# A two-layer hybrid backbone on one core: norms in two parts of the tokens, gating constants loaded during the FFN, two gates first in the merge, output splits ahead of the additions

## The reference: what is computed

```
h  = rms(x) * (1 + scale1) + shift1              # per token norm, per channel modulation (norm 1)
o  = four token mixers of h @ w_in               # neighbourhood, latent, spatial gating, grouped attention
y  = sum_i sigmoid(h @ w_gate[i] + b_gate[i]) * (o[i] @ w_branch[i])        # the merge
x  = x + gate1 * (y @ w_out)                     # the out stage
h2 = rms(x) * (1 + scale2) + shift2              # norm 2
x  = x + gate2 * (silu(g) * a) @ w_down          # a, g = depthwise convolution of h2 @ w_up
```

## Time and profile before

| | |
|---|---|
| Time, median of 3 runs | 2396.87 us (2396.68 to 2398.68) |
| Profiled execution, its own time | 2399.9 us |
| Profiled execution, span | 2398.2 us |
| TensorE busy in it | 95% of the span |
| VectorE, ScalarE, GpSimd busy | 56%, 40%, 7% |
| Granted TensorE clock, mean | 0.985 |
| Moved by DMA | 221.21 MB, mean 92 GB/s |

### The profile page before, as it was taken

One profiled execution on the slowest core, in us unless ns is written; L12 is line 12 of the kernel. 1 busy time (PEld: TensorE's weight loads), 2 busy tenths in 40 slices (PEclk: granted clock), 3 DMA queues, 4 the chain that ended last, 5 costly groups with the idle time before them and its releaser, 6 DMA issues.

```text
span 2398.2 us, 34895 instructions
## 1 busy us (share of the span) xinstructions
PE 2284.1 (95%) x12816; PEld 1891.5 (79%) x12816; DVE 1339.0 (56%) x1877; ACT 955.2 (40%) x1389; POOL 164.9 (7%) x169
## 2 busy tenths in 40 slices
PE   6999988999999989999999979999999998999999
PEld 5788766788888868888888857776778886888887
DVE  6555566466667465425534555556745565645545
ACT  3554556422223253213312345545643334423332
POOL 2113010000000000000000001130100000000000
PEclk9999999999999999999999999999999998999999
DMA  7112110243343211111111131120135542222223
GB/s 281 44 53 71 36 40 19 97 141 132 131 142 126 109 50 65 62 62 62 61 62 62 62 133 44 63 79 18 49 128 177 176 166 90 97 96 97 96 97 114
DMA packets 58621, 221.21 MB, mean 92 GB/s; under 512 B 6720, under 2 KB 6720, under 8 KB 57872
## 3 DMA queue, kind: packets, MB, share of 16 engines
q1 hardware_dynamic: 44496, 160.46, 19.1%
q0 software_dynamic: 14016, 59.26, 6.9%
HBM read 214.45 MB, written 5.24 MB: 92 GB/s over the span
## 4 chain that ended last, share of the span: by engine, by line
PE 88%; DVE 4%; ACT 3%; issue 2%; DMA 2%; ACTq 0%; SPq 0%; DVEq 0%
PE PS L584 85%; PE PS L862 3%; ACT TM L1014 1%; DVE F_lo L1344 1%; ACT XY L1014 1%; DVE ROPE L1400 1%; DMA ROPE<-w_mod 1%; DVE XY L1347 0%; ACT F_hi L1014 0%; DMA SGX<-sg_bs 0%; DVE W_lo L1344 0%; ACT W_hi L1014 0%; DMA XY<-x_spill 0%; DVE XY L1563 0%; DVE TM L1347 0%
## 5 line engine op out<-in xcount | busy, mean ns | idle before, releaser
L584 PE MATMUL PS<-H_hi,W_hi 128*128 128x512 f32 x2240 | 677.7, 359 | 45.1 <-DVE H_lo L1344 26.1
L584 PE MATMUL PS<-H_hi,W_lo 128*128 128x512 f32 x2240 | 670.2, 356 | 0.0
L584 PE MATMUL PS<-H_lo,W_hi 128*128 128x512 f32 x2240 | 668.2, 355 | 0.0
L1344 DVE TENSOR_TENSOR W_lo<-W_st,W_hi 128x1024 fp32r<-128x1024 f32 x278 | 343.7, 1237 | 555.9 <-ACT W_hi L1014 554.4
L1014 ACT ACTIVATE W_hi<-W_st 128x1024 fp32r<-128x1024 f32 x278 | 293.5, 1057 | 820.4 <-PE PS L584 811.2
L584 PEld LDWEIGHTS PS<-H_hi,W_hi 128*128 128x128 f32 x2240 | 370.3, 190 | 121.5 <-issue 44.0
L584 PEld LDWEIGHTS PS<-H_lo,W_hi 128*128 128x128 f32 x2240 | 367.6, 189 | 63.4 <-issue 2.2
L584 PEld LDWEIGHTS PS<-H_hi,W_lo 128*128 128x128 f32 x2240 | 368.5, 189 | 61.8
L584 PE MATMUL PS<-F_hi,W_hi 128*128 128x512 f32 (+1 forms) x952 | 290.1, 359 | 15.9 <-DVEq L442 5.4
L584 PE MATMUL PS<-F_hi,W_lo 128*128 128x512 f32 (+1 forms) x952 | 289.6, 359 | 0.0
L584 PE MATMUL PS<-F_lo,W_hi 128*128 128x512 f32 (+1 forms) x952 | 287.0, 356 | 0.0
(11 more groups left out here) (130 smaller groups left out, 2089.1 us busy)
## 6 DMA issues: line engine op xcount, KB each, us to landing
W_st<-w_all SPq DMA_DIRECT2D x278, 512.0 KB, 3.4
RA<-w_mod POOLq DMA_DIRECT2D x40, 512.0 KB, 3.7
TM<-w_mod POOLq DMA_DIRECT2D x40, 512.0 KB, 3.7
RA<-w_ada SPq DMA_DIRECT2D x8, 512.0 KB, 8.9
XY<-bias_na POOLq DMA_DIRECT2D x2, 1792.0 KB, 8.0
RA<-w_mod SPq DMA_DIRECT2D x6, 512.0 KB, 8.4
XY<-x_in SPq DMA_DIRECT2D x4, 768.0 KB, 11.7
x_spill<-XY POOLq DMA_DIRECT2D x1, 3072.0 KB, 11.0
```

The source lines that it names most:

```text
L584: return nc.tensor.matmul(o, lhsT, rhs, start=start, stop=stop)
L1344: return nc.vector.tensor_tensor(o, a, b, f)
```

## The change

1. `norm` is taken apart. The tokens are divided into two parts (`halves`): at width 768 first the 256 context tokens, then the 512 latent ones; at width 512 two parts of 256. At norms behind output tiles, the last two output tiles (6 and 7) are computed first for the first part (signal `out_half`), then for the second part. Root, products and low parts of the first part are issued by ScalarE and VectorE among the remaining work of these tiles. `E7_BEHIND` and `SPLIT_BEHIND` say after which k the last tile's addition and a split stand.
2. Each k of a norm has one VectorE product with both the root and the scale (`product`), one ScalarE operation that adds the shift and rounds (`high`), and one VectorE operation (`low`) that adds the shift and subtracts the high part. The scratch is a ring of three (`NU`).
3. `two_early_tiles` goes over the first part for both tiles (the second tile wholly behind the first when `late`), then over the second part with the lag of three. The squares of the second part are multiplied inside it.
4. GpSimd issues the gating constants of layer 1 before, and PAR and the spill after, a wait for the last addition; TensorE waits for the constants only ahead of the gating products.
5. The first two gate blocks of a merge come before its first branch block (`MERGE_HEAD`), and `begin` of TensorE stands behind them.
6. In `out_tiles` with a norm behind them all splits stand ahead of the addition and the square.

```diff
+MERGE_HEAD = (1, 2, 0, 3, 4, 5)
+def halves(w):
+    return [(SEQ, CTX), (0, SEQ)] if w == T else [(0, SEQ // 2), (SEQ // 2, SEQ // 2)]
+E7_BEHIND = {T: 4, SEQ: 2}
+SPLIT_BEHIND = {T: 1, SEQ: 0}
...
@@ gpsimd
-                if l:
-                    begin(pool, p0, "pe", "act", "dve")
-                    pool.dma_start(PAR[:, :], par[l]).then_inc(S["par_loaded"], 16)
-                    pool.dma_start(x_spill, XY[:, :]).then_inc(S["x_spilled"], 16)
                 wait(pool, "mask_step", NHEAD * l)
+                wait(pool, "sg_lo", 2 * l)
                 pool.dma_start(SGG, sg_gain[l]).then_inc(S["sg_loaded"], 16)
...
+                if l:
+                    pool.wait_ge(S["down_add"], KT * len(GROUPS) + 2)
+                    pool.dma_start(PAR[:, :], par[l]).then_inc(S["par_loaded"], 16)
+                    pool.dma_start(x_spill, XY[:, :]).then_inc(S["x_spilled"], 16)
@@ tensor, two_early_tiles
+                for h, (s0, sn) in enumerate(halves(w)):
+                    lag = KT if late and h == 0 else 3
+                    for step in range(KT + lag):
+                        for t, k in ((0, step), (1, step - lag)):
...
+                        if late and h == 0 and step == 2:
+                            seven_squares(w, 1)
+                        if late and h == 0 and step == 4:
+                            eighth_square(w, 1)
@@ tensor, merge
+                        if first(i) and u == 0:
+                            for r in range(2):
+                                gate(i, u, r, b + r)
+                            begin(pe, ph, "act", "dve")
+                            branches(i, u, b + 2)
@@ tensor, out_tiles
+                for h, (s0, sn) in enumerate(halves(w)):
+                    for t in (KT - 2, KT - 1):
+                        if h == 0:
+                            have_block(b0 + t)
+                        pe.wait_ge(S[free], base[free] + t - 1 + 2 * h)
+                        for k in range(k_tiles):
...
+                            if h == 1 and t == KT - 2 and k == 2:
+                                base.advance(**norm_counts())
+                                seven_squares(w, 0)
+                                eighth_square(w, 0)
+                        ins.then_inc(S["block_done" if h else "out_half"], 1)
@@ scalar, out_tiles
+                square(KT - 2, 0)
+                load_root_table()
+                square(KT - 1, 0)
+                root(w, 0)
+                for k in range(KT):
+                    high(w, 0, k, tail)
+                    if k == SPLIT_BEHIND[w]:
+                        used(0, 2, b0 + KT - 2)
+                    if k == 1:
+                        square(KT - 2, 1)
+                    if k == E7_BEHIND[w]:
+                        square(KT - 1, 1)
+                        used(0, 2, b0 + KT - 1)
+                root(w, 1)
+                for k in range(KT):
+                    high(w, 1, k, tail)
@@ vector, out_tiles
-                        early = reloads and first(i)
+                        early = tail is not None
...
+                residual(KT - 2, 0)
+                seventh_square(0)
+                residual(KT - 1, 0)
+                root(w, 0)
+                product(w, 0, 0, sc)
+                for k in range(KT):
+                    if k + 1 < KT:
+                        product(w, 0, k + 1, sc)
+                    low(w, 0, k, sh)
+                    if k == 0:
+                        residual(KT - 2, 1)
+                    if k == SPLIT_BEHIND[w]:
+                        used(0, 2, b0 + KT - 2)
+                    if k == 1:
+                        seventh_square(1)
+                    if k == E7_BEHIND[w]:
+                        residual(KT - 1, 1)
+                used(0, 2, b0 + KT - 1)
+                root(w, 1)
+                product(w, 1, 0, sc)
+                for k in range(KT):
+                    if k + 1 < KT:
+                        product(w, 1, k + 1, sc)
+                    low(w, 1, k, sh)
@@ vector, merge
+                        head = first(i) and u == 0
+                        for v in range(3 if head else 1):
+                            used(i, 10, b + v)
```

More of the change, by code:

```diff
@@ L354, in bank, with stat_at @@
             return PS[:, 512 * i:512 * i + 512]
+        def stat_at(w, h):
+            s0, sn = halves(w)[h]
+            at = 3072 + s0 if w == T else (2560, 3584)[h]
+            return PS[:, at:at + sn]
         def colmajor(ap):
@@ L1033, in squares_of_x, with root, high @@
                     split_hi(b, b, 16)
-            def norm(ph, w, sc, sh):
+            def root(w, h):
+                s0, sn = halves(w)[h]
+                act.wait_ge(S["ss"], base["ss"] + h + 1)
+                op(NY0[:, s0:s0 + sn], stat_at(w, h), ACT.Abs_reciprocal_sqrt, bias=EPSB).then_inc(S["y0"], 1)
+                act.wait_ge(S["y0"], base["y0"] + h + 1)
+                op(NRT[:, s0:s0 + sn], NY0[:, s0:s0 + sn], ACT.Square).then_inc(S["y_sq"], 1)
+            def high(w, h, k, sh):
+                s0, sn = halves(w)[h]
+                act.wait_ge(S["norm_u"], base["norm_u"] + KT * h + k + 1)
+                op(H_hi[:, k, s0:s0 + sn], NU[k % 3][:, s0:s0 + sn], ACT.Identity,
+                   bias=MOD[:, stream(s0), sh + k:sh + k + 1]).then_inc(S["norm_hi"], 1)
@@ L1054, in norm @@
-                base.advance(**norm_counts())
+                for h in range(2):
+                    root(T, h)
+                for h in range(2):
+                    for k in range(KT):
+                        high(T, h, k, SH1)
+                base.advance(**norm_counts(False))
             def in_stage(l, ph):
@@ L1226, in split_y, with copies, sigmoid @@
                     op(F_hi[:, k, 0:w], X3[:, k, 0:w], ACT.Copy).then_inc(S["y_hi"], 1)
+                def copies(i, u, b):
+                    for r in range(NBR):
+                        if r < NBR - 1:
+                            act.wait_ge(S["sub_gemm"], i * 6 + (base["sub_gemm"] + 3 * u + r + 1))
+                        else:
+                            used(i, 10, b)
+                        wait(act, "gate_mul", i * 8 + (base["gate_mul"] + NBR * (u - 1) + r + 1)
+                             if not first(i) or u else 0)
+                        op(BR[:, r, 0:w], pair(2 + r % 2, w), ACT.Copy).then_inc(S["br_copy"], 1)
+                def sigmoid(i, u, r, b):
+                    used(i, 10, b)
+                    wait(act, "gate_mul", i * 8 + (base["gate_mul"] + NBR * u + r - 1)
+                         if not first(i) or u or r > 1 else 0)
+                    op(SIG[:, r % 2, 0:w], pair(r % 2, w), ACT.Sigmoid,
+                       bias=PAR[:, bass.ds(i * 2 + (u + C_BG + KT * r), 1)]).then_inc(S["gate_sig"], 1)
                 def body(i, last):
@@ L1430, in in_stage, with first_norm @@
+            def first_norm(ph):
+                begin(dve, ph, "pe", "act")
+                for h in range(2):
+                    root(T, h)
+                for h in range(2):
+                    for k in range(KT):
+                        product(T, h, k, SC1)
+                        if k:
+                            low(T, h, k - 1, SH1)
+                    low(T, h, KT - 1, SH1)
+                base.advance(**norm_counts(False))
             def in_stage(l, ph):
@@ L1678, in body @@
                         ins.then_inc(S[name], 1)
-                        if squares and u == 0 and not first(i):
+                        if tail is not None and u == 0 and not first(i):
                             dve.wait_ge(S["sq"], i * 2 + (base["sq"] + 1))
@@ L1691, in body @@
                             used(i, 2, b0 + u, stop=final and last_phase)
-                def last(i):
-                    return isinstance(i, int) and i == KT // 2 - 1
-                repeat(dve, KT // 2, body, peel_last=last_phase or squares)
+                if tail is None:
+                    repeat(dve, KT // 2, body, peel_last=last_phase)
+                    done[0] += KT
+                    base.advance(**{name: KT})
+                    return
+                repeat(dve, KT // 2 - 1, body)
@@ new lines, in out_tiles, with residual @@
+                sc, sh = tail
+                def residual(t, h):
+                    s0, sn = halves(w)[h]
+                    if h:
+                        dve.wait_ge(S["block_done"], b0 + t + 1)
+                    else:
+                        dve.wait_ge(S["out_half"], base["out_half"] + t - KT + 3)
+                    x = X3[:, t, s0:s0 + sn]
+                    stt(x, pair(t % 2)[:, s0:s0 + sn], MOD[:, stream(s0), gate + t:gate + t + 1], x, ALU.mult, ALU.add
+                        ).then_inc(S[name], 1)
@@ L1751, in _ @@
                     ada()
[L1752 removed]
+                    one_plus_scale(SC1)
                 end(dve, "dve")
```

277 lines of the change are left out of this document (152 added, 125 removed).

## The result

The changed kernel takes 2367.3 us (median of 4 executions, 2365.8 to 2370.6) where the kernel before takes 2397.8 on the same chip: ratio 0.990, 95% interval 0.988 to 0.992, a gain of 30.4 us where 25.4 were forecast. It was measured twice more beside the kernel before: 2369.8 against 2394.0 (ratio 0.990, 0.988 to 0.992) and 2372.7 against 2392.2 (0.991, 0.990 to 0.993), gains of 24.3 and 19.5 us. So the gain is between 19 and 31 us, and part of the first 30 belongs to that comparison and not to the change; where it sits is the last point of the explanation.

The account below looks back on a forecast made before the run. TensorE was taken as the bound, busy 2284.1 of 2398.2 us, so only its gaps count. Gains 8.5 + 8.1 + 1.4 + 2.0 + 5.9 + 1.0 - 1.5 = 25.4 give a median of 2371.5 us, range 2364 to 2384.

Parts of the forecast that it names:

- second norm, layer 0: Halved norm behind layer 0's output tiles: from tile 5's end to the next tile 41.4 us instead of 49.9, gain 8.5.
- first norm, layer 1: Layer 1's first norm, halved and without the wait for gating constants: 42.6 us instead of 50.7, gain 8.1.
- first norm, layer 0: Norm without output tiles to hide under: next tile starts at 75.5 instead of 77.44, gain 2.0 us.
- merge entries: Two gates first in each merge: phase signal waits of 3.0 and 2.4 us shrink to about 0.4, gains 2.5 and 2.0.
- VectorE caught up in the merge: In the merge VectorE starts modulation 10 us later but catches up before branch copies need buffers; otherwise up to 5 us lost.
- splits first: Last down stage of layer 0: the 1.6 us wait for W_lo becomes 0.6 us for residual 0, gain 1.0.
- clock lost in the norms: Halved stretches idle TensorE in short pieces, so its clock may drop: 0 to 1.7 us a norm, 1.5 taken in all.
- B: Rival: thin norm stretches leave TensorE at 1.2 GHz through the early tiles; 2413 us; chance 0.07 with other losses.
- A: Rival: VectorE's queue bounds the norms harder, 0.5 us per 256-column step instead of 0.42; gain 15, 2382 us; chance 0.17.
- C: Rival: the norm's second part ends no earlier than now, only the merge gains 4 to 7; 2391 us; chance 0.08.
- D: Rival: shorter waits inside the first half, first halves entirely hidden; gain 32 to 36, 2362 us; chance 0.06.
- The rule against the change: Skill advice for VectorE pieces of at least 512: norms better whole, halving only a loss of 1.9 us per norm.

Follow-up runs that it names:

- the fourth run: Changed kernel with one more unused 128x256 VectorE product ahead of each of eight first-part products, in the three norms behind output tiles; 2375.3 us.
- the third: Changed kernel with ScalarE's square of tile 7 and the split behind it moved one place back, VectorE's list as it was; 2366.1 us.
- the tenth run: Changed kernel with the second silu right behind the first and three modulation tiles of VectorE ahead of its wait for the merge's third block; 2364.1 us.
- the fifth run: The changed kernel measured again, unedited, beside the kernel before; 2369.8 us against 2394.0.
- the eleventh run: The changed kernel measured a third time, unedited, beside the kernel before; 2372.7 us, ratio 0.9912.
- the first run: Kernel before with only the three gating constant loads moved ahead of the wait for the FFN's end; 2389.1 us against 2393.1.
- four such edits: On the changed kernel: ScalarE's square and split later, odd residuals before splits, two x tiles reloaded early, merge silu and modulation tiles earlier; together 2360.1 us.

## Why the prediction was right

The forecast (2371.5, range 2364 to 2384) held, and at most places for its reasons. That the terms below add up to 24.9 where the forecast has 25.4 is in part luck: 1.5 us for the clock that did not lengthen the norms cancel against 1.3 us for a stop in the merge that the forecast did not have, and 1.1 too much for the first norm against smaller misses the other way. By its own terms, in us, all from the profiled executions:

```
term                               forecast   measured
second norm, layer 0                 8.5        8.4    (49.9 -> 41.5)
first norm, layer 1                  8.1        8.1    (50.7 -> 42.6; constants 4.5, halving 3.6)
second norm, layer 1                 1.4        1.2    (34.8 -> 33.6)
first norm, layer 0                  2.0        0.9    (28.7 -> 27.8)
merge entries                        4.5        4.9    (2.95 + 2.44 idle -> 0.26 + 0.27)
clock at the merge's entry           1.4        1.6
VectorE caught up in the merge       0         -1.3    (472.72 instead of about 465)
splits first                         1.0        1.1    (1.64 -> 0.52)
clock lost in the norms             -1.5        0      (see below)
```

*The walks.* Second norm of layer 0: the wait for tile 5's pair ended at 3.6 (forecast 3.8), residual 7 ran at 18.7 (18.7), the hole lay behind k=4, the second part's first `H_lo` was ready at 28.2 (28.6), the end came at 41.5 (41.4). This part was right because it walked both in-order lists operation by operation; the fourth run shows that the list of VectorE is the price, the third that ScalarE's is close behind it.

*First norm of layer 0*: the term was mis-sized, 0.9 us where 2.0 were forecast. The next tile does start at 75.17, 2.3 us earlier than at 77.44, but 1.4 of that is the start of the whole program: TensorE stopped ahead of the norm at 47.33 in the one execution and at 48.74 in the other. In the kernel before and in the changed one:

```profile
57.20 0.98 PE L584 MATMUL PS<-H_hi,W_hi 128*128 128x512 f32 x2 [8.46 <-DVE H_lo L1344]
```

```profile
52.85 0.55 PE L611 MATMUL PS<-H_hi,W_hi 128*128 128x256 f32 x1 [5.52 <-DVE H_lo L1459]
```

From the start of that idling (48.74; 47.33) to the next tile it is 28.7 and 27.8 us; later executions of the changed kernel have 27.8 as well. The walk has 26.8 on this scale (75.5 - 48.74), 1.0 too short. Its two roots in a row end at 3.0 (51.7) and in the trace at 3.8, its lows at 21.2 (69.9) and in the trace at 21.8, and behind the lows 6.0 us pass where the walk has 5.6. That 75.17 lies so near its 75.5 is luck.

*Merge*: the entry was right, the sentence "it catches up before the branch copies of the next u need their buffers" was not. The buffers were not the next thing needed, the weight split of the sixth block was; the tenth run shows it.

*The clock.* The 1.5 us loss did not come in layer 0 (granted clock 1.00 in every stretch of that norm, with idle pieces of up to 0.8 us). It did come in the two norms of layer 1 (first fence), but not in every execution: the fifth run, same program, has 1.00 in both (second fence, the short norm):

```profile
1413.00:1418.00 5.00, 3.81 (x15) 2.82 (x14) 4.00 (x7) 2.87 (x6) 0.11 (x1) 0.72 1.00 416
...
1996.00:2000.00 4.00, 4.00 (x16) 3.74 (x17) 3.82 (x9) 2.42 (x5) 0.00 (x0) 0.50 0.00 0
```

```profile
1996.00:2000.00 4.00, 2.98 (x18) 2.13 (x18) 3.81 (x8) 2.22 (x5) 0.00 (x0) 1.00 0.00 0
```

Yet the short norm is 33.6 us long in both, and the first norm of layer 1 42.6 in both, since VectorE's list is the longer one: the low clock cost nothing. So B was right in kind and wrong in size: a piecewise fed TensorE sometimes falls to 1.2 GHz, for some 3 us at 1415 and 7 us at 1996 (an estimate from the granted clock in windows of 1 us), and not for the whole of the early tiles. The Trainium skill, "TensorE: Matmul & The Clock Gate", section "HAM oscillation — how this bites in real kernels", describes a kernel throttled anew after each of its waits, which are waits for DMA and several times longer than those here. The norm of layer 0, with seven waits of 0.39 to 0.76 us and the clock at 1.00, does not behave so; to take the section for a rule on every wait, as B does, went too far.

*The other rivals.* A falls: a 256-column step of VectorE's list took 0.40 us, not 0.5. C falls: the second part's first low came at 28.2 and the norm still ended 8.4 us earlier. D is near by the median (30.4, it has 32 to 36) and not by the terms. The rule against the change falls too, though its price was set too low: before, VectorE's 768-column operations start 0.87 us apart (56.09 and 56.96), so a k cost 1.74 us whole and costs 2.12 in parts (2 x 0.40 and 2 x 0.66), 3.0 us a norm and not 1.9. VectorE is busy 9.6 us longer in all, and each norm is shorter.

*Why 30 and not 25.* The terms measured add up to 24.9; the spans of the two profiled executions differ by 29.3. Of the remaining 4.4, 3.2 are the pitch of long stretches, which the same program shows in two values, 0.347 and 0.354 us a pair. Stretches 1680, 672 and 768 of the changed kernel (the first's are above, its x768 took 133.36; here the fifth and the eleventh run, whose x768 took 133.36 too):

```profile
474.43 291.45 PE PS L611 x1680
...
860.22 118.94 PE PS L611 x672
...
1046.58 135.91 PE PS L611 x768
```

```profile
476.58 297.05 PE PS L611 x1680
...
867.92 116.72 PE PS L611 x672
```

The slow pitch costs 5.6 us in the first, 2.2 in the second, 2.5 in the third. The profiled execution of before had slow stretches worth some 11.4 us, that of the changed kernel 8.2: 3.2 of the difference. That they do not come of the change is borne out by the first run, which is the kernel before up to the end of layer 0's merge: its stretch of 1920 took 334.62 us where that of before took 340.96.

Nor do the pitches fall wholly anew each time. The eleventh run has those of the first execution in all six stretches of layer 0, the fifth differs in four. And in the 13 profiled executions with the long matmul first, the stretch behind a slow one of 384 was fast in 15 cases of 15, behind a fast one of 384 slow in 9 of 11. What sets the pitch is open.

The last 1.2 us are a balance. TensorE's earlier stop ahead of the first norm gives 1.4. From the next tile to the entry of the merge the changed kernel took 2.2 us more (355.5 against 353.2; the fifth run 353.7), 1.7 of them at 298, with a granted clock of 0.70 to 0.88. Other stretches gave some 2 us back; one is in the kernel before at 1984, with a clock of 0.57. They are not settled one by one. The forecast took a pitch of 0.354 from the earlier trace rows as a constant of the kernel; it is one of two.

## What to carry to other kernels

An in-order list is worth walking operation by operation, ScalarE's beside VectorE's: here three walks of 34 to 43 us came out within 0.2, and a fourth missed by 1.0. When work is moved ahead of a wait, ask for every later item of the waiting engine's list, not for the one that seems most urgent: the stop in the merge came from a weight split that stood behind eight products for which TensorE did not wait. And measure an edit of 1 or 2 us between two landmarks of one trace: the medians of four to six executions here could not tell three of four such edits from nothing, and gave the fourth seven times its size, though together they take some 9 us off by the trace (12.6 by the medians).

## What the runs showed of the hardware

- Two pitches of one and the same stretch: 0.347 and 0.354 us per 512 + 256 matmuls, 2% apart, kept to the end of the stretch. In 13 profiled executions of kernels with the long matmul first, 35 of 78 long stretches were slow, and the one behind a slow stretch of 384 matmuls never was. With the short matmul first no stretch was slow, in the one execution profiled, but for the part of one that still had the long matmul first. The Trainium skill, "TensorE: Matmul & The Clock Gate", gives in the section "Wait — 56ns, not 53.3ns?" a start-to-start of N / 2.4 GHz plus 2.5 ns once warm; for 768 columns in two matmuls that would be an estimate of 0.325, and both pitches here are above it.
- VectorE's two-operand steps with a per-partition scalar overlap their tails: the 256-column one shows 0.48 us and the next starts 0.40 later, the 512-column one 0.75 and 0.66.
- Low clock after short idle pieces comes in one execution and not in another of the same program, behind the same idle piece of 1.69 us (1996 to 2000: 0.50 and 1.00).
